# A rebuilt beginning and reordered seams in a four-layer hybrid trunk kernel

## The chip, the cores and the metric

One core of one Trainium2 chip runs the whole step. The metric is device time in microseconds. Before the change the median of three runs is 2044.71 us (2044.56 to 2045.04).

## What is computed

384 tokens of width 1024 (128 context, 256 latent) pass through four layers: pooling mixer, Mamba-2 SSD, Conformer convolution, attention, each followed by a ConvFFN. Each sub-layer is

```python
h = rms_norm(x, g_pre) * (1 + scale) + shift
x = x + gate * rms_norm(mixer(h), g_post)
```

where shift, scale and gate are six vectors of a layer, `silu(cond) @ w_mod + b_mod`, one set for the context tokens and one for the latent ones. The pooling mixer takes, for four groups of 256 columns, the mean over a window of 2, 4, 8 or 16 rows less the row itself, and multiplies each group with a 256 x 256 weight and a scale. Everything is float32.

## The kernel before

Five engines each have their own hand-written list of instructions, tied by semaphores. Tokens stand in three blocks c = 0 (context), 1 and 2 (latent). Matmuls are done in split form: an operand is rounded to fp32r (`w_hi`, `h_hi`) and the rest kept (`w_lo`, `h_lo`), and a product is three matmuls (hi x hi, lo x hi, hi x lo; L1825 to L1827 in `tile`, L1861 to L1863 in `out_part`, L2274 to L2276 in the pooling product). Weights come in chunks of 512 KB into four `raw` slots; ScalarE rounds a chunk (`round_to`, L880), GpSimd (POOL) and VectorE make half of its low part each (`low_to`, L752 and L1267; for conf and qkv weights POOL makes all of it). A chunk number n stands for the first chunk of the next product.

Modulation vectors are made by TensorE from 1 MB pieces, four to a vector (`mod_piece`, L1796), and finished on VectorE (`mod_vector`, `coefficient`). Five vectors are made in the start, three inside ffn_in0 and its transition, three in each later seam (one in the last), where their pieces fill TensorE's time. `FILLS` says how many stand before turn 1 and turn 2.

**Start** (`pool_mix` on TensorE, L1715 to L1757 on VectorE, L1193 to L1217 on ScalarE). `pool_m` holds the window matrices. TensorE multiplies them with ones (`sums`) and then with the normalised rows, one bank for each of eight column groups k, alternating banks 6 and 7. ScalarE scales (L1208), VectorE adds the shift (L1743), ScalarE rounds (L1215), VectorE takes the low part (L1752); `pooled_v` has two buffers. The order of SHIFT0's pieces is behind k = 1, that of GATE0's behind k = 5. The gate coefficients, a 16 x 128 block, are turned to a row by TensorE, copied by ScalarE (`copy_row`), written to HBM (`rows_dram`) and read back into all partitions (`gb`), from ScalarE's queue. Then comes the product and `transition0`.

**Seam t** (t = 0 to 6, the end of sub-layer t; event e = 3t + c). For each block: `first` (square sums of the product, ScalarE), `weigh` (product times gate, L1324; in t = 0 and 4 a scale or bias first, L1319), `residual` (L1333), `second` (square sums of x, L908), `unit` (x normalised, L1340), `turn_unit` (eight transposes on TensorE into pair[3], L1818), `unit_stage` (scale and shift; four groups on ScalarE, L921, four on VectorE, L1352), `unit_high` (L930), `unit_low` (four groups on POOL, L759, four on VectorE, L1360). The lists of all three engines are in `transition` and `transition0`. `in_start` waits for the low parts of all blocks, then tile 0 of the next product starts. SP issues nearly all loads in one queue, in program order, with the waits that free the slots.

## Time and profile before

| | us |
|---|---|
| median of 3 runs | 2044.71 |
| the profiled execution | 2046.58 |
| its span | 2044.8 |
| TensorE busy in it | 1935.7 |
| VectorE, ScalarE, POOL busy | 1191.7, 924.0, 713.5 |

The page cuts the span into 40 slices (51 us each) and gives the busy tenths of each engine:

```profile
PE   6699999999998989999999998899999979899998
PEclk8799999999999989999999999999999989899999
DMA  9764346433330137533374655533365413333342
```

PE is TensorE, PEclk the clock it was granted in tenths of full speed, DMA the busy share of the DMA engines. The first two slices hold the start; the other places below 9 hold the seams and the scan and attention stages. Rows below are of four views: the chain that ended last, the waits, the timeline (start, duration, engine, line, operation, and in brackets the idle time before and what released it) and windows (busy time in chosen stretches, with the clock).

### The profile page before, as it was taken

The page shows a single profiled execution, that of the slowest core. Times are in us where ns is not written, and L with a number is a line of the kernel's source. Part 1 is how long each engine was busy: PE and PEld are TensorE (multiplying, and loading weights), DVE is VectorE, ACT ScalarE, POOL GpSimd, SP SyncE. Part 2 cuts the span into 40 slices and gives each one's busy share as a digit, 9 for nine tenths or more (in the row PEclk, how much of TensorE's full clock was granted, in tenths as well). Part 3 has the DMA queues.
Part 4 walks back from the last instruction along what each step waited for, and adds up shares of the span by engine and source line. Part 5 has one row for each costly group of instructions (what it writes and reads, how often), then busy time and mean ns, then how long its engine had stood idle before and what let it go on. Part 6 is the DMA issues. An engine that isn't in the chain of part 4 may idle for free.

```text
span 2044.8 us, 29870 instructions
## 1 busy us (share of the span) xinstructions
PE 1935.7 (95%) x11679; PEld 1713.0 (84%) x11679; DVE 1191.7 (58%) x1789; ACT 924.0 (45%) x1566; POOL 713.5 (35%) x515
## 2 busy tenths in 40 slices
PE   6699999999998989999999998899999979899998
PEld 3589998799996767999987956899987867799986
DVE  3557761566626675777615844777724684777722
ACT  3444442554546645444424325544424444544422
POOL 0223324333335553333344722333343521333342
PEclk8799999999999989999999999999999989899999
DMA  9764346433330137533374655533365413333342
GB/s 399 319 247 135 124 164 246 169 123 124 97 134 27 48 134 305 187 125 125 116 246 172 207 155 202 211 124 124 113 240 182 174 40 114 112 128 124 124 132 72
DMA packets 80316, 324.29 MB, mean 159 GB/s; under 512 B 9009, under 2 KB 17713, under 8 KB 66609
## 3 DMA queue, kind: packets, MB, share of 16 engines
q1 hardware_dynamic: 78496, 319.42, 44.6%
q10 hardware_dynamic: 1680, 2.96, 0.4%
q8 instruction: 94, 1.54, 0.3%
q14 instruction: 46, 0.37, 0.1%
HBM read 317.24 MB, written 5.10 MB: 158 GB/s over the span
## 4 chain that ended last, share of the span: by engine, by line
PE 81%; DVE 7%; ACT 5%; issue 3%; POOL 2%; DMA 2%; SPq 0%; DVEq 0%; ACTq 0%; POOLq 0%
PE pair L1825 18%; PE pair L1827 17%; PE pair L1826 17%; PE pair L1861 7%; PE pair L1862 7%; PE pair L1863 7%; DVE x L1333 2%; PE pair L1982 2%; PE pair L2076 1%; DMA raw<-in_pool 1%; ACT junk L908 1%; PE pair L1796 1%; DVE wk L1324 1%; PE pair L1987 1%; PE pair L2203 1%
## 5 line engine op out<-in xcount | busy, mean ns | idle before, releaser
L752 POOL TENSOR_TENSOR w_lo<-raw,w_hi 128x512 fp32r<-128x512 f32 (+1 forms) x375 | 587.8, 1569 | 1133.2 <-ACT w_hi L880 1133.1
L1825 PE MATMUL pair<-h_hi,w_hi 128*128 128x386 f32 (+1 forms) x2008 | 687.5, 342 | 13.2 <-POOL h_lo L759 10.5
L1827 PE MATMUL pair<-h_hi,w_lo 128*128 128x386 f32 (+1 forms) x2008 | 682.6, 340 | 0.0
L1826 PE MATMUL pair<-h_lo,w_hi 128*128 128x386 f32 (+1 forms) x2008 | 682.0, 340 | 0.0
L1267 DVE TENSOR_TENSOR w_lo<-raw,w_hi 128x512 fp32r<-128x512 f32 x339 | 411.3, 1216 | 325.5 <-ACT w_hi L880 325.4
L880 ACT ACTIVATE w_hi<-raw 128x1024 fp32r<-128x1024 f32 x375 | 392.9, 1050 | 292.6 <-PE pair L1863 225.6
L1825 PEld LDWEIGHTS pair<-h_hi,w_hi 128*128 128x128 f32 (+1 forms) x2008 | 380.0, 189 | 22.2 <-POOL h_lo L759 16.7
L1826 PEld LDWEIGHTS pair<-h_lo,w_hi 128*128 128x128 f32 (+1 forms) x2008 | 380.5, 189 | 0.9
L1827 PEld LDWEIGHTS pair<-h_hi,w_lo 128*128 128x128 f32 (+1 forms) x2008 | 380.0, 189 | 0.3
L1416 DVE SCALAR_TENSOR_TENSOR acc<-pair,taps,acc 128x385 f32<-128x385 f32 x176 | 108.9, 619 | 207.4 <-ACT acc L984 207.4
L984 ACT ACTIVATE acc<-pair,taps 128x386 f32<-128x386 f32 x176 | 117.3, 666 | 224.7 <-PE pair L1827 224.7
L1862 PE MATMUL pair<-w_hi,g 128*128 128x512 f32 x528 | 208.5, 395 | 0.0
L1863 PE MATMUL pair<-w_lo,g 128*128 128x512 f32 x528 | 208.4, 395 | 0.0
L1861 PE MATMUL pair<-w_hi,g 128*128 128x512 f32 x528 | 208.3, 395 | 0.0
L1861 PEld LDWEIGHTS pair<-w_hi,g 128*128 128x128 f32 x528 | 99.2, 188 | 23.4
L1862 PEld LDWEIGHTS pair<-w_hi,g 128*128 128x128 f32 x528 | 99.2, 188 | 23.3
L1863 PEld LDWEIGHTS pair<-w_lo,g 128*128 128x128 f32 x528 | 99.2, 188 | 23.4
L982 ACT ACTIVATE g<-gate 128x386 fp32r<-128x386 f32 x84 | 44.3, 527 | 163.2 <-DVE gate L1434 163.2
L1423 DVE SCALAR_TENSOR_TENSOR acc<-pair,taps,acc 128x385 f32<-128x385 f32 x176 | 108.5, 617 | 3.2
L1058 ACT ACTIVATE mod_raw<-pair,shift 128x128 f32<-128x128 f32 x192 | 53.7, 378 | 14.3 <-PE pair L1987 14.2
L759 POOL TENSOR_TENSOR h_lo<-stage,h_hi 128x512 fp32r<-128x512 f32 x21 | 32.0, 1522 | 79.5 <-ACT h_hi L930 79.5
L1818 PE MATMUL pair<-ident,wk 128*128 128x128 f32 x168 | 27.0, 313 | 29.9 <-ACT stage L921 12.3
(286 smaller groups left out, 2128.0 us busy)
## 6 DMA issues: line engine op xcount, KB each, us to landing
raw<-in_ffn_in SPq DMA_DIRECT2D x176, 512.0 KB, 3.5
raw<-in_ffn_out SPq DMA_DIRECT2D x88, 512.0 KB, 3.5
mod_raw<-in_w_mod SPq DMA_DIRECT2D x36, 1024.0 KB, 6.8
mod_base<-in_w_mod SPq DMA_DIRECT2D x31, 1024.0 KB, 7.1
mod_more<-in_w_mod SPq DMA_DIRECT2D x18, 1024.0 KB, 20.4
raw<-in_ssd_conv SPq DMA_DIRECT2D x32, 512.0 KB, 3.5
raw<-in_ssd_z SPq DMA_DIRECT2D x16, 512.0 KB, 3.5
raw<-in_ssd_out SPq DMA_DIRECT2D x16, 512.0 KB, 3.8
```

The costliest lines, as they stand in the source:

```text
L752: pool.tensor_tensor(w_lo[:, m % SLOTS, 0:w], raw[:, m % SLOTS, 0:w], w_hi[:, m % SLOTS, 0:w].bitcast(F32), ALU.subtract).then_inc(w_low_p ...
L880: act.activation(w_hi[:, m % SLOTS, 0:w], raw[:, m % SLOTS, 0:w], ACT.Copy).then_inc(w_rounded, 1)
L984: act.activation(acc[:, j % 4, :], tile_bank(j)[:, 0:COLS], ACT.Identity, scale=taps[:, l, j, 1:2], bias=taps[:, l, j, 3:4]).then_inc(acc_ ...
L1267: vec.tensor_tensor(w_lo[:, m % SLOTS, w0:w1], raw[:, m % SLOTS, w0:w1], w_hi[:, m % SLOTS, w0:w1].bitcast(F32), ALU.subtract).then_inc(w_ ...
L1416: vec.scalar_tensor_tensor(out=acc[:, j % 4, 1:COLS], in0=b[:, 0:COLS - 1], scalar=taps[:, l, j, 0:1], in1=acc[:, j % 4, 1:COLS], op0=ALU. ...
L1423: vec.scalar_tensor_tensor(out=acc[:, j % 4, 0:COLS - 1], in0=b[:, 1:COLS], scalar=taps[:, l, j, 2:3], in1=acc[:, j % 4, 0:COLS - 1], op0= ...
L1825: ten.matmul(to, wh, h_hi[:, k, cols], start=k == 0, stop=False, skip_group_check=True)
L1826: ten.matmul(to, wh, h_lo[:, k, cols], start=False, stop=False, skip_group_check=True)
L1827: ins = ten.matmul(to, wl, h_hi[:, k, cols], start=False, stop=k == KD - 1, skip_group_check=True)
L1861: ten.matmul(to, hi[:, k, cols], wh, start=first, stop=False)
L1862: ten.matmul(to, lo[:, k, cols], wh, start=False, stop=False)
L1863: ins = ten.matmul(to, hi[:, k, cols], wl, start=False, stop=last)
```

## The change

Start: `pool_m` keeps only the 136 columns that a block of 128 rows can reach for each latent block (643 columns become 401). Four pooling buffers and four banks (6, 7, 0, 1); rounding and low part of a group come two groups late; ScalarE rounds the pool weights behind four evacuations; SHIFT0's pieces stand behind k = 3, GATE0's behind all groups. The gate row is no longer sent through HBM: TensorE multiplies the gate column, broadcast over 128 columns, with the identity (`spread_gate`), once for each of the two streams, between the thirds of the product, and ScalarE copies the result into `gb`. The product times pool scale of block 2 goes into `h_rows`, dead by then. Turned units of t = 0 go to three different bank pairs. Pieces of vectors 3 and 4 stand around turn 0. SP loads p20 to p23 ahead of the tables.

Seams: POOL makes only the low part of block 0, VectorE all of block 1 and both halves of block 2; block 2 is rounded in halves and tile 0 starts after the first half, its k = 4 waiting for the second; the first chunk's rounding and low part come later in all three lists; `FILLS` changes from (3, 7) to (1, 6).

The core of the diff:

```diff
-POOL_W = LAT0 + 2 * (LAT + 1)
+REACHED = P + max(WINDOWS) // 2
+POOL_W = LAT0 + 2 * REACHED
+POOL_DEPTH = 4
-FILLS = {12: (3, 7), 4: (1, 3)}
+FILLS = {12: (1, 6), 4: (1, 3)}
...
@@ sync @@
             load_to(4)
+            load_ends(0, *range(MOD_PIECES))
             for to, name in ((taps, "taps"), (ssd_taps, "ssd_taps"), (dt_rows, "dt_rows"), (ssd_cols, "ssd_cols")):
...
@@ gpsimd @@
             def transition(t, n):
-                low_to(n + 1)
                 unit_low(t, 0)
-                unit_low(t, 1)
-                low_to(n + 2)
-                unit_low(t, 2)
                 low_to(n + 4)
...
@@ scalar @@
+            def gate_copy(s):
+                act.wait_ge(gate_spread, s + 1)
+                act.activation(gb[:, s, :], pair[3][:, :], ACT.Copy).then_inc(gate_copied, 1)
             def transition0(n):
+                gate_copy(0)
                 first(0, 0)
+                gate_copy(1)
                 first(0, 1)
                 second(0, 0)
                 second(0, 1)
-                round_to(n + 1)
+                first(0, 2)
+                round_to(n + 2)
+                second(0, 2)
                 unit_stage(0, 0)
-                first(0, 2)
                 unit_high(0, 0)
                 unit_stage(0, 1)
-                second(0, 2)
                 unit_high(0, 1)
-                round_to(n + 2)
                 unit_stage(0, 2)
                 unit_high(0, 2)
                 round_to(n + 4)
@@ transition(t, n) @@
                 first(t, 1)
-                round_to(n + 1)
                 unit_stage(t, 0)
                 second(t, 1)
+                unit_high(t, 0)
                 first(t, 2)
-                unit_high(t, 0)
+                unit_stage(t, 1)
                 second(t, 2)
-                unit_stage(t, 1)
                 unit_high(t, 1)
-                round_to(n + 2)
+                round_to(n + 1)
                 unit_stage(t, 2)
...
-            for k in range(KD + 1):
+            for k in range(KD + 2):
                 if k < KD:
                     act.wait_ge(pooled, k + 1)
-                    if k >= 2:
-                        act.wait_ge(pooled_lo, k - 1)
-                    if k == 0:
+                    if k >= POOL_DEPTH:
+                        act.wait_ge(pooled_lo, k - POOL_DEPTH + 1)
+                    if k == POOL_DEPTH:
                         round_to(2)
...
-                if k:
-                    act.wait_ge(pooled_shifted, k)
+                if k >= 2:
+                    act.wait_ge(pooled_shifted, k - 1)
...
@@ vector @@
             def transition0(n):
+                mod_vector(2)
+                coefficient(0, 1)
+                before_weigh(0, 0)
                 weigh(0, 0)
+                before_weigh(0, 1)
+                residual(0, 0)
                 weigh(0, 1)
-                residual(0, 0)
+                residual(0, 1)
+                unit(0, 0)
+                before_weigh(0, 2)
+                unit(0, 1)
                 mod_vector(3)
                 coefficient(0, 2)
+                weigh(0, 2)
+                residual(0, 2)
                 mod_vector(4)
...
+                unit(0, 2)
+                unit_stage(0, 0)
+                unit_stage(0, 1)
+                unit_low(0, 0)
+                unit_low(0, 1)
+                unit_stage(0, 2)
                 low_to(n + 1)
...
                 unit_low(0, 2)
                 low_to(n + 4)
@@ transition(t, n) @@
                 unit(t, 1)
-                low_to(n + 1)
                 weigh(t, 2)
                 residual(t, 2)
+                unit_stage(t, 1)
                 unit_low(t, 0)
-                unit_stage(t, 1)
                 unit(t, 2)
                 unit_low(t, 1)
-                low_to(n + 2)
                 unit_stage(t, 2)
+                low_to(n + 1)
                 unit_low(t, 2)
...
@@ tensor @@
+                def spread_gate(s):
+                    for k in range(KD):
+                        ins = ten.matmul(pair[3][:, k * P:(k + 1) * P], coef[:, 0, 1, s, k:k + 1].broadcast_to([P, P]),
+                                         ident[:, :], start=True, stop=True, skip_group_check=True)
+                    ins.then_inc(gate_spread, 1)
...
-                turn_gate(0)
...
                     if c < 2:
                         ins.then_inc(out_done, 1)
-                ten.wait_ge(pooled_scaled, KD)
-                for p in range(3 * MOD_PIECES, START_VECTORS * MOD_PIECES):
+                        if c == 0:
+                            ten.wait_ge(coef_ready, 2)
+                            ten.wait_ge(pooled_scaled, KD)
+                        else:
+                            ten.wait_ge(gate_copied, 1)
+                        spread_gate(c)
+                for p in range(3 * MOD_PIECES, 4 * MOD_PIECES - 1):
                     mod_piece(p)
-                ten.wait_ge(mod_read, START_VECTORS)
+                ten.wait_ge(gate_copied, 2)
                 turn_unit(0, 0)
+                for p in range(4 * MOD_PIECES - 1, START_VECTORS * MOD_PIECES):
+                    mod_piece(p)
+                ten.wait_ge(pre_ready, 2)
                 turn_unit(0, 1)
+                ten.wait_ge(pre_ready, 3)
                 turn_unit(0, 2)
+                ten.wait_ge(stage_act, 1)
+                ten.wait_ge(stage_dve, 1)
                 fill(0, 0, MOD_PIECES)
```

## Rows read from the trace of the kernel before

**Rows 1.** The page, part 4: share of the chain that ended last, by engine.
```profile
PE 81%; DVE 7%; ACT 5%; issue 3%; POOL 2%; DMA 2%; SPq 0%; DVEq 0%; ACTq 0%; POOLq 0%
```

**Rows 2.** Waits of PE, 0 to 110 us: line, awaited, us in total, times, longest.
```profile
PE pair L1818 <- DVE wk L1340: 10.0, 2, 6.9
...
PE pair L1818 <- DVE stage L1352: 5.3, 1, 5.3
...
PE pair L2274 <- DVE h_lo L1752: 4.1, 1, 4.1
```

**Rows 3.** Waits of PE, 370 to 1800 us.
```profile
PE pair L1818 <- ACT stage L921: 12.3, 5, 4.8
...
PE pair L1825 <- POOL h_lo L759: 10.5, 5, 4.3
...
PE pair L1825 <- DVE w_lo L1267: 2.6, 1, 2.6
```

**Rows 4.** The chain that ended last, up to tile 0: start us, us, what.
```profile
57.14 11.01 DMA gb<-rows_dram
...
69.38 1.23 DVE wk L1319
...
97.84 0.42 PE pair L1825
```

**Rows 5.** Windows: us, busy us by engine, granted clock, DMA share, GB/s.
```profile
85.00:90.00 5.00, 1.94 (x8) 1.57 (x8) 4.93 (x11) 4.13 (x9) 1.20 (x1) 0.50 0.71 295
```

**Rows 6.** Timeline, 24 to 41 us: start us, us, engine, line, [idle before, releaser].
```profile
24.67 0.39 PE L2234 MATMUL pair<-pool_m,ones 128*128 128x129 f32 x2
...
32.20 1.07 PE L1796 MATMUL pair<-mod_more,cond 128*32 128x256 f32 x16 [0.26 <-DMA mod_more<-in_w_mod]
...
38.92 0.74 ACT L1208 ACTIVATE stage<-pair,coef 128x129 f32<-128x129 f32 x2 [0.69 <-DVE h_lo L1752]
...
39.69 0.75 DVE L1743 SCALAR_TENSOR_TENSOR stage<-wk,modc,stage 128x129 f32<-128x129 f32 x2 [0.86 <-ACT stage L1208]
...
40.36 0.55 DVE L1752 TENSOR_TENSOR h_lo<-stage,h_hi 128x386 fp32r<-128x386 f32 x1
...
41.01 0.73 ACT L1208 ACTIVATE stage<-pair,coef 128x129 f32<-128x129 f32 x2 [0.94 <-DVE h_lo L1752]
```

**Rows 7.** Windows of PE alone in the pooling product: us, busy us, clock, DMA share, GB/s.
```profile
53.40:58.00 4.60, 4.60 (x22) 0.50 1.03 429
...
59.00:64.00 5.00, 5.00 (x44) 1.00 1.01 424
```

**Rows 8.** DMA issues at 19.6, 45.6, 46.3, 67.1 us: KB, us to landing.
```profile
mod_more<-in_w_mod SPq DMA_DIRECT2D x1, 1024.0 KB, 24.9
...
mod_raw<-in_w_mod SPq DMA_DIRECT2D x1, 1024.0 KB, 22.5
...
raw<-in_ffn_in SPq DMA_DIRECT2D x1, 512.0 KB, 23.4
...
mod_more<-in_w_mod SPq DMA_DIRECT2D x1, 1024.0 KB, 15.2
```

**Rows 9.** Timeline of the seam t = 1, 384 to 404 us.
```profile
384.06 1.30 POOL L752 TENSOR_TENSOR w_lo<-raw,w_hi 128x512 fp32r<-128x512 f32 x1 [10.74 <-ACT w_hi L880]
...
384.11 2.33 DVE L1333 SCALAR_TENSOR_TENSOR x<-wk,inv,x 128x1024 f32<-128x1024 f32 x1
...
387.89 1.93 PE L1796 MATMUL pair<-mod_raw,cond 128*32 128x256 f32 x32
...
398.99 1.36 DVE L1352 TENSOR_SCALAR stage<-pair,coef,modc 128x128 f32<-128x128 f32 x4
...
401.53 0.69 DVE L1360 TENSOR_TENSOR h_lo<-stage,h_hi 128x512 fp32r<-128x512 f32 x1 [1.19 <-ACT h_hi L930]
...
403.76 0.41 PE L1825 MATMUL pair<-h_hi,w_hi 128*128 128x386 f32 x1 [2.50 <-POOL h_lo L759]
```

**Rows 10.** Windows of PE alone, tile 0 behind the seam t = 2.
```profile
822.80:826.00 3.20, 3.20 (x12) 0.51 0.35 105
```

More of the change, by code:

```diff
@@ L296, in build_trunk @@
         pool_sums = flat_wk[:, 0:len(WINDOWS) * COLS].rearrange("p (g n) -> p g n", g=len(WINDOWS))
-        pooled_v = [flat_stage[:, k * 512:k * 512 + COLS] for k in range(2)]
+        pooled_v = [flat_stage[:, k * 512:k * 512 + COLS] for k in range(POOL_DEPTH)]
         def c_part(v, d, h):
@@ L928, in unit_high @@
                 act.wait_ge(stage_act, e + 1)
-                act.wait_ge(stage_dve, e + 1)
-                act.activation(h_hi[:, :, cols], stage[:, e % 2, :, :], ACT.Copy).then_inc(h_hi_ready, 1)
+                if c < 2:
+                    act.wait_ge(stage_dve, e + 1)
+                    act.activation(h_hi[:, :, cols], stage[:, e % 2, :, :], ACT.Copy).then_inc(h_hi_ready, 1)
+                else:
+                    for half in range(2):
+                        ks = slice(4 * half, 4 * half + 4)
+                        if half:
+                            act.wait_ge(stage_dve, e + 1)
+                        act.activation(h_hi[:, ks, cols], stage[:, e % 2, ks, :], ACT.Copy).then_inc(h_hi_ready, 1)
+            def gate_copy(s):
+                act.wait_ge(gate_spread, s + 1)
+                act.activation(gb[:, s, :], pair[3][:, :], ACT.Copy).then_inc(gate_copied, 1)
             def transition0(n):
+                gate_copy(0)
                 first(0, 0)
+                gate_copy(1)
                 first(0, 1)
@@ L1358, in unit_low @@
                 e, cols = event(t, c), slice(AT[c], AT[c] + P)
-                vec.wait_ge(h_hi_ready, e + 1)
-                vec.tensor_tensor(h_lo[:, 4:, cols], stage[:, e % 2, 4:, :], h_hi[:, 4:, cols].bitcast(F32),
-                                  ALU.subtract).then_inc(h_lo_dve, 1)
+                for half in range(2) if c == 2 else (1,):
+                    ks = slice(0, KD) if c == 1 else slice(4 * half, 4 * half + 4)
+                    vec.wait_ge(h_hi_ready, highs_made(t, c, half))
+                    vec.tensor_tensor(h_lo[:, ks, cols], stage[:, e % 2, ks, :], h_hi[:, ks, cols].bitcast(F32),
+                                      ALU.subtract).then_inc(h_lo_dve, 1)
             def transition0(n):
+                mod_vector(2)
+                coefficient(0, 1)
+                before_weigh(0, 0)
                 weigh(0, 0)
+                before_weigh(0, 1)
+                residual(0, 0)
                 weigh(0, 1)
-                residual(0, 0)
+                residual(0, 1)
+                unit(0, 0)
+                before_weigh(0, 2)
+                unit(0, 1)
                 mod_vector(3)
                 coefficient(0, 2)
+                weigh(0, 2)
+                residual(0, 2)
                 mod_vector(4)
-                residual(0, 1)
-                unit(0, 0)
-                unit(0, 1)
-                low_to(n + 1)
-                weigh(0, 2)
-                unit_stage(0, 0)
-                residual(0, 2)
-                unit_low(0, 0)
-                unit_stage(0, 1)
-                unit(0, 2)
-                unit_low(0, 1)
-                low_to(n + 2)
-                unit_stage(0, 2)
+                unit(0, 2)
[4 more added lines that the diff above has]
+                unit_stage(0, 2)
+                low_to(n + 1)
                 unit_low(0, 2)
@@ L1817, in turn_unit, with tile @@
                 for k in range(KD):
-                    ins = ten.transpose(pair[3][:, k * P:(k + 1) * P], wk[:, e % 2, k * P:(k + 1) * P], ident[:, :])
+                    ins = ten.transpose(turned_pair(t, c)[:, k * P:(k + 1) * P], wk[:, e % 2, k * P:(k + 1) * P], ident[:, :])
                     if k % 4 == 3:
                         ins.then_inc(unit_turned, 1)
-            def tile(to, n, w, cols):
+            def tile(to, n, w, cols, behind=None):
                 for k in range(KD):
+                    if behind is not None and k == 4:
+                        ten.wait_ge(h_lo_dve, lows_on_dve(behind, 2, 1))
                     wh, wl = (v[:, n % SLOTS, k * w:(k + 1) * w] for v in (w_hi, w_lo))
```

201 lines of the change are left out of this document (111 added, 90 removed).

## The prediction

> **What bounds the kernel now.** I read the page first: TensorE carries 81% of the chain that ended last [rows 1]. Inside the stages between the seams it has nothing to wait for, so this change can only win or lose where TensorE stands still or runs slowly. The list of its waits says where. In the first 98 us, before tile 0 of ffn_in0 starts, it waits four times for the work around the pooling mixer and the first transition [rows 2]. Behind that it waits in the six later seams (t = 1 to 6): 12.3 us in five waits before a turn of a unit (L1818), and 10.5 + 2.6 us in six waits before tile 0 of the next product [rows 3]. The chain then tells what ends last at the start: the gate row, written to HBM and read back (the reading alone 11.01 us, to 68.15), so that the first weighing stands until then, and a ping-pong of VectorE and ScalarE up to tile 0 at 97.84 [rows 4]. The DMA engines are full until about 88 us and then idle [rows 5]: they are the second thing to watch.
>
> I number the modulation pieces p0 to p19 (vector i is p4i to p4i+3), p20 to p23 being the first of the next phase.
>
> **The start, step by step.**
>
> Smaller pool_m. Its columns go from 643 to 401, so 1286 KB become 802 KB; the 0.50 MB at about 415 GB/s (295 at a share of 0.71 [rows 5]) bring all later transfers 1.2 us forward. TensorE's matmuls over it get shorter, beside other work: nothing on the path.
>
> Pooling. The last piece of SHIFT0 is used from 32.20 to 33.27 [rows 6] and its vector takes 0.8 more; less 1.2 us, the first shift can run at 32.9. Today the third group is only evacuated at 38.92 [rows 6], because ScalarE rounds two weights first, at the landing of the pool weights, and then each column group k goes evacuation, shift, high part, low part, at 2.1 us a group (38.92 to 41.01, L1208) because there are two buffers [rows 6]. With four buffers and the low part two groups late, the engines overlap. VectorE has 8 x (0.75 + 0.55) + 1.3 for the weights' low part = 11.7 us, ScalarE 8 x (0.74 + 0.52) + 2.1 for two roundings. I followed the order of both: ScalarE is held at h_hi(0) until 33.8, rounds from 35.7 to 37.7, and the rest runs at 1.26 us a group; last low part 46.0, against 53.2 now. Vector 2's pieces on TensorE (p8 to p11) now come behind all groups; p11, issued at 19.6, lands 24.9 later [rows 8], less 1.2 at 43.3, and is used by 44.4: no new wait. Gain so far 7.2 us.
>
> Product and gate. The product's first third ran at a granted clock of 0.50, the 1.2 GHz level: 22 matmuls in 4.6 us, against 44 in 5.0 later [rows 7]. Again 24 at 0.21, 5.1 us, to 51.2. Then spread_gate(0), eight fp32 matmuls of 128 columns. The nearest row is L2234, 129 columns, two records and 0.22 us a matmul [rows 6], so 1.7 us (3.5 at the half clock). Then c = 1 (2.8), spread (1.7), c = 2 (2.8): TensorE is done at 60.5, not 64.1. ScalarE copies the gate from 53.05 (1.05 us), then squares. This replaces the round trip through HBM: the first weighing goes at 55.4 instead of 68.2. What is late next is VectorE's list: before_weigh and weigh 1.23 each [rows 4], and of the same width residual 1.28 with a reciprocal of 0.2, unit 0.95. In the new order that puts unit(0,0) at 63.7 and unit(0,1) at 65.7.
>
> Last column block. SCALE1's vector needs p15 (65.7), weigh(0,2) runs 66.6 to 67.8, residual to 69.2. ScalarE stands in front of second(0,2) with round_to(n+2): the ffn_in0 weights, issued from 46.3, landed near 69.7 and 71 [rows 8]; they are 1.2 us sooner by pool_m and 2.5 us by the row of 1 MB that is no longer written to gb, so 66 and 67.3, rounded by 68.7. So second(0,2) runs 69.25 to 70.7, unit(0,2) is ready at 71.7. SHIFT1 needs p19, issued at 45.6 and landed at 68.1 now [rows 8], 64.5 after: its vector is made at 70.0, not last. VectorE then does unit_stage(0,0) to 73.0, stage(0,1), the low parts and stage(0,2), a stage 1.36, a low part of four groups 0.69 [rows 9], ending 79.2, the moved low part of chunk n to 79.9, the first half of unit_low(0,2) at 80.5. Tile 0 at 80.6 against 97.84: 17.2 us.
>
> DMA order. p20 to p23 are now queued ahead of the tables; p21 still waits on SP until p12 is used, and behind SP stand tables and weights n+2 and n+3. p23, issued at 67.1, landed at 82.3 [rows 8]; without 2.0 MB ahead of it (pool_m, gb, tables) it lands near 77 and TensorE has used it at 78. Cover is 2.5 us; later than that, tile 0 starts one for one later. The weights for tile 2 land near 80, needed at 89.
>
> Clock. TensorE is now paced by DMA from 72.8 to 78 and idle to 80.6. Where TensorE was mostly idle the granted clock was 0.50 [rows 5], and the product behind it had its first third at that level [rows 7], which cost it 24 x 0.09 = 2.2 us. Today tile 0 follows on pieces that run without a gap. I charge it what the product paid, a little up: 2.5. Start: 17.2 - 2.5 = 14.7 us. Bounds: 17.2 with a warm clock; 9 if the p19/p23 landings or ScalarE's order cost 3 to 5 us more.
>
> **The seams t = 1 to 6.** The change takes the low part of c = 1 from POOL wholly to VectorE (+0.65 us there), halves the last high and low part so tile 0 starts after the first half, takes the rounding of chunk n from before unit_stage(t,0) to behind unit_high(t,1), and gives turn 1 one fill piece in place of three. I take t = 1 as the pattern [rows 9]. VectorE's residual took 2.33 us beside POOL's w_lo [rows 9] and 1.28 alone: 1.05 us back. unit_stage(0) runs at 385.3, not 386.4; unit(2) is ready at 394.65, not 395.5. Then: unit_low(1) with 8 groups to 395.9, unit_stage(2) to 397.2, low part of chunk n to 397.9, half a low part to 398.55. VectorE and ScalarE would let tile 0 go at 398.6 against 403.76. But TensorE has its own work from the product's end at 387.89: 15.87 us passed to tile 0, of which 2.94 were waits, so 12.9 us of pieces and turns. With 0.3 for the one short gap left before turn 2 it is ready at 401.1. So the bound changes from POOL's h_lo to TensorE itself, and such a seam gives its waits less 0.3, not the 5 us of the chain: t = 1 2.6; and, with the waits of [rows 3] split by seam, t = 3 (3.0 us of waits) 2.7; t = 5 (3.1) 2.8; t = 2 (3.5) 3.2. At t = 2 the granted clock was 0.51 in the first 3.2 us of tile 0, behind the wait [rows 10]; half of that, 1.7 with the edges, goes too if the wait goes: 4.9.
>
> t = 4 is longer because a bias is added first: unit(2) comes at 1283.6 instead of 1285.8, turn 2 still waits 2.4 us and turn 1 1.5, then six pieces: tile 0 at 1290.1, not 1294.1; less 0.5 for clock: 3.5. t = 6 has only four pieces (phase 7 is one vector), so the chain itself counts: 5.1 us; the clock of its tile 0 I leave as it is. Sum of seams 2.6 + 4.9 + 2.7 + 3.5 + 2.8 + 5.1 = 21.6 us. Bounds: 14 (clock unchanged, another 0.7 us gap a seam) to 25.
>
> What is moved, and its cover. POOL's w_lo of n and n+1 come later (396.8 and 400.6 in the t = 1 pattern); tile 0 is at 401.1, tile 1 4.3 us on. For conf_in and qk POOL makes the whole 1024 columns, 2.4 us a chunk, still under 4.3 us a tile. Pieces 9 to 11 of a seam are loaded into slots that pieces 0 to 2 free; piece 2 is used at 391.7, 1.1 us later than now, lands some 7 us behind and is needed at 400.2: 1.3 us of cover. Row indices, semaphores and psum banks cost nothing.
>
> The Trainium skill, SBUF — State Buffer (Who interferes with whom), says that a VectorE instruction with two SBUF inputs and a GpSimd one exclude each other for a whole instruction. The residual beside w_lo (2.33 against 1.28) agrees. That rule also speaks against the change: unit_low(t,1) on VectorE and w_lo of chunk n on POOL now meet at 395.5. By it VectorE loses up to 1.3 us there; in five seams TensorE's own 12.9 us hide that, in t = 6 they don't, and the sum would be 1.3 us smaller.
>
> **The sum.** 14.7 + 21.6 = 36.3 us. The profiled execution took 2046.58 with a span of 2044.8; the median of the runs is 2044.71. Against the span 2008.5, and I take the same for the median.
>
> **Rivals.**
> A. The start stays tied to DMA: p19 or p23 lands 4 to 6 us later than I count, or ScalarE's roundings hold second(0,2) for longer. For: DMA share is 1.0 throughout, and SP's queue stands behind matmuls [rows 5, 8]. Against: 2 MB less ahead. Start 9, seams 21.6: 2014.
> B. The seams give almost nothing, because the turns wait again: new order on ScalarE puts unit_high(0) before first(2) (1.05 us) and second(2) behind unit_stage(1). If that comes back as wait at turn 2, only start and 5 us remain: 2025. Against: unit(2) has 0.3 us to lose and TensorE 2.5 us of slack at the end.
> C. Clock. The seams' and the start's tile 0 run warm, with all chain gains: 17.2 + 25: 2002. Against: the clock of 0.50 from 80 us on [rows 5], with the same idle stretches ahead. The Trainium skill, TensorE: Matmul & The Clock Gate (What's actually happening), has the clock halved after idling; the trace agrees.
> D. Slower: VectorE becomes the bound in the seams. It gets 0.65 us of low part, and each meeting with POOL costs 1.05 to 1.3. It decides once a seam's chain, 398.6 by my count, ends later than 403.76, and to eat the start too it must be 2.5 us beyond that in all six: 7.6 us more VectorE time a seam, six meetings with POOL where I see one. It would give 2050.
> E. Nothing happens, gains and losses cancel: 2044.7.
>
> **Chances.** Forecast (2004 to 2013) 0.60; A 0.17; B 0.10; C 0.08; D 0.03; E 0.02. The range takes in A, C and the near part of B: 1999 to 2023. A measurement of this kernel can tell 0.2% (4 us) from none: faster 0.95, same 0.02, slower 0.03.
>
> **What would show it.** Right: no gb transfer at the start; first weigh (now L1324) near 55; tile 0 of ffn_in0 near 80 with 0.32 us between matmuls first; in seams 1, 2, 3, 5 no wait before tile 0 and a TensorE-bound seam of some 13.2 us; in t = 6 a start 5 us nearer to the product's end. Wrong: TensorE waiting for DMA on a piece just before tile 0, a wait of over 1 us before turn 2, or VectorE rows of 2 us in the seams.

## The result and the profile after

| | median | runs | profiled span | granted clock |
|---|---|---|---|---|
| before | 2044.88 | 2044.56 to 2046.06 | 2044.8 | 0.976 |
| after | 2007.79 | 2007.7 to 2008.61 | 2006.0 | 0.985 |
| forecast | 2008.5 | range 1999 to 2023 | | |

All in us. The ratio is 0.9818 with a 95% interval of 0.9801 to 0.9836: 37.1 us less by the medians and 38.8 by the spans, where 36.3 had been forecast. (The median of before in this table is over four runs: the three named at the beginning and one more.)

TensorE's share of the chain that ended last is up from 81% [rows 1] to 87%. Page of the changed kernel, part 4:

```profile
PE 87%; DVE 5%; ACT 2%; issue 2%; DMA 2%; POOL 1%; SPq 0%; DVEq 0%; POOLq 0%; ACTq 0%
```

TensorE's waits in the changed kernel, the answers to [rows 2] (0 to 110 us) and to [rows 3] (350 to 1800 us); columns: line, awaited, us in total, times, longest:

```profile
PE pair L1870 <- DVE wk L1388: 2.0, 2, 1.7
PE pair L1879 <- DVE h_lo L1409: 1.8, 1, 1.8
```

```profile
PE pair L1870 <- DVE wk L1388: 8.7, 8, 2.8
...
PE pair L1879 <- DVE h_lo L1409: 0.9, 1, 0.9
```

Lines have moved: the turn of a unit is now L1870 (L1818 before), the first matmul of a product L1879 (L1825), a modulation piece L1848 (L1796). In the seams TensorE had 25.4 us of waits in eleven places [rows 3], and 2.1 more in three for VectorE's wk, not shown there. They have become 9.6 in nine, and the wait for POOL's h_lo ahead of tile 0 is gone: the only one left there is 0.9 us, for VectorE, in the seam t = 6.

The span splits at the first matmul of each phase's tile 0 (each row from one profile). This ledger sets the forecast's terms beside what came:

| stretch, ending with tile 0 of | before | after | gained | forecast |
|---|---|---|---|---|
| start to ffn_in0 | 97.84 | 79.76 | 18.1 | 17.2 |
| ssd_conv (t = 1) | 305.92 | 305.13 | 0.8 | 2.6 - 2.5 |
| ffn_in1 (t = 2) | 418.79 | 415.75 | 3.0 | 3.2 |
| conf_in (t = 3) | 298.17 | 294.10 | 4.1 | 2.7 + 1.7 |
| ffn_in2 (t = 4) | 173.38 | 170.58 | 2.8 | 3.5 |
| qk (t = 5) | 296.44 | 293.82 | 2.6 | 2.8 |
| ffn_in3 (t = 6) | 165.17 | 160.29 | 4.9 | 5.1 |
| the end | 289.09 | 286.57 | 2.5 | 0 |

The seams themselves can be cut out more narrowly, from TensorE's first modulation piece behind the product to tile 0. For t = 1 to 6 that was 15.9, 16.4, 15.9, 20.8, 16.0 and 15.8 us, and is 13.6, 13.5, 13.6, 18.1, 13.4 and 11.4: 17.4 us less in all. What the stretches behind the start gain beyond that, 3.3 us, is put down to the clock and to the scatter of a profile.

The start of the changed kernel, the last part of the chain of work up to tile 0 (start us, us, what); the columns of [rows 4]:

```profile
45.75 0.55 PE pair L2326
50.36 1.78 PE pair L2292 x16
54.96 1.80 PE pair L2292 x16
...
78.46 0.60 DVE w_lo L1300
79.06 0.61 DVE h_lo L1409
79.76 0.54 PE pair L1879
```

The 11 us of reading gb back [rows 4] are no longer there; two spreads of 1.8 us by TensorE (L2292) stand in their place, and VectorE's last list ends last.

### The profile page after: what moved, and what is told of

It reads as the page before. It is cut to its first block, busy times and chain, and to the rows that moved or that the text cites. A ratio compares the mean times of both kernels' runs of the same rounds, so it can differ in the third digit from the quotient of the medians.

```text
span 2006.0 us, 29908 instructions
## 1 busy us (share of the span) xinstructions
PE 1927.0 (96%) x11710; PEld 1705.9 (85%) x11710; DVE 1183.8 (59%) x1796; ACT 927.1 (46%) x1574; POOL 692.1 (35%) x501
## 4 chain that ended last, share of the span: by engine, by line
PE 87%; DVE 5%; ACT 2%; issue 2%; DMA 2%; POOL 1%; SPq 0%; DVEq 0%; POOLq 0%; ACTq 0%
PE pair L1879 18%; PE pair L1881 18%; PE pair L1880 18%; PE pair L1911 8%; PE pair L1912 8%; PE pair L1913 8%; PE pair L1848 2%; PE pair L2032 2%; PE pair L2126 1%; DMA mod_base<-in_w_mod 1%; DMA pool_m<-in_pool_m 1%; PE pair L2253 1%; PE pair L2037 1%; PE pair L1870 1%; PE pair L2046 1%
## 5 line engine op out<-in xcount | busy, mean ns | idle before, releaser
L1879 PE MATMUL pair<-h_hi,w_hi 128*128 128x386 f32 (+1 forms) x2008 | 686.6, 342 | 2.7 <-DVE h_lo L1409 2.7
L1300 DVE TENSOR_TENSOR w_lo<-raw,w_hi 128x512 fp32r<-128x512 f32 x339 | 405.8, 1200 | 325.3 <-ACT w_hi L908 325.2
L1879 PEld LDWEIGHTS pair<-h_hi,w_hi 128*128 128x128 f32 (+1 forms) x2008 | 378.9, 189 | 11.5 <-issue 10.1
L1037 ACT ACTIVATE xbc<-pair,ssd_taps 128x386 f32<-128x386 f32 x32 | 21.6, 674 | 72.7 <-PE pair L1881 72.7
L1486 DVE TENSOR_TENSOR gate<-sil,acc 128x386 f32<-128x386 f32 x88 | 53.8, 611 | 0.0
```

The lines of the kernel that those rows point to most:

```text
L1300: vec.tensor_tensor(w_lo[:, m % SLOTS, w0:w1], raw[:, m % SLOTS, w0:w1], w_hi[:, m % SLOTS, w0:w1].bitcast(F32), ALU.subtract).then_inc(w_ ...
L1879: ten.matmul(to, wh, h_hi[:, k, cols], start=k == 0, stop=False, skip_group_check=True)
```

## The experiments

All are edits of the changed kernel. "By segment" means the stretches of the ledger, each from one profile. Kernels that share a start had tile 0 of ffn_in0 anywhere from 79.5 to 81.1 us, so that a single start is good to about 1 us.

### Start or seams

The start as changed, and for t of 1 and up the old order on all three lists and the old shares (VectorE's list, changed back in the same way, is not shown):

```
+ if t == 0: unit_low(t, 0)
+ else: low_to(n + 1); unit_low(t, 0); unit_low(t, 1); low_to(n + 2); unit_low(t, 2)      (GpSimd)
+ round_to(n + 1)                                              (ScalarE, before the seam's first unit)
- FILLS = {12: (1, 6), 4: (1, 3)}
+ FILLS = {12: (3, 7), 4: (1, 3)}
```

> The new beginning with the old seams t = 1 to 6 (lists of all engines, POOL's share, whole last block, FILLS (3, 7)). My theory: the two halves of the change add up, the start being worth 38.8 us minus the 22.4 us that the traces give to the seams: 2044.8 - 16.4 = 2028.4 us, with the old waits of TensorE before turn 2 and tile 0 back (some 27 us in all with turn 0 and 1). Rival (the seams give little, and the start all): 2010 to 2015. Rival (a slower rounding of tile 0's weights shifts loads, so that the parts don't add): off the sum by over 3 us.

Measured: 2026.96 (ratio 0.9916, interval 0.990 to 0.993; span 2027.4). So the start is worth 17.9 us and the seams 19.2 by medians, 17.4 and 21.4 by spans; forecast 14.7 and 21.6. (The profiled execution was the slowest of the four, 2.2 us above their median.) Most of the old waits are back, 22.7 of the 25.4 us:

```profile
PE pair L1879 <- ACT stage L955: 12.3, 5, 4.8
PE pair L1888 <- POOL h_lo L791: 10.4, 5, 3.8
```

(TensorE's waits of this kernel, 350 to 1800 us; compare [rows 3].)

### The start: four buffers, narrow pool_m, gate row

```
- POOL_DEPTH = 4
+ POOL_DEPTH = 2                          (and the low part one group late, not two)
```

> The changed kernel with two pooling buffers and two banks, rounding and low part one group late as before; all else of the new beginning stays. My theory: a group takes 2.1 us again instead of 1.1 to 1.3, from the third or fourth on, so the product starts 5 to 6 us later (near 51 instead of 45.75) and, since VectorE and ScalarE end last from there to tile 0, nearly all of it reaches tile 0 (84 to 86 instead of 79.76): 2012 to 2014 us. Rival (the DMA landings p19 and p23 end last, so the buffers were worth little): within 2 us of the changed kernel.

Measured: tile 0 at 84.26, 4.5 us later; median 2009.82. The whole is only 2.0 us slower, since the stretch to ffn_in1 came out 2.2 us shorter by TensorE's clock (below).

```
- REACHED = P + max(WINDOWS) // 2
+ REACHED = LAT + 1
- POOL_LAT = [(LAT0, LAT0), (LAT0 + REACHED, COLS - REACHED)]
+ POOL_LAT = [(LAT0, LAT0), (LAT0 + REACHED, LAT0)]
```

> The changed kernel with pool_m at 643 columns again. 0.5 MB more are loaded ahead of most of the start. My theory: all landings come 1.2 us later; the first shifts and the product wait for p7 and start about 1 us later, tile 0 about 1 us: 2009 us. Rival (cover on the DMA side is thin, p23 lands behind the low parts): over 2 us. Rival (no effect, a chain that doesn't touch the loads): below 0.3.

Measured: tile 0 at 82.92, 3.2 us later; median 2010.20. The rival's "over 2" came, but not by the late landing that it named. TensorE's timeline between 20 and 36 us, the wide kernel first and then the changed one (start us, us, engine, line, operation):

```profile
20.97 0.80 PE L2283 MATMUL pair<-pool_m,ones 128*128 128x129 f32 x2 [5.27 <-DMA pool_m<-in_pool_m]
...
28.57 1.03 PE L2286 MATMUL pair<-pool_m,h_rows 128*128 128x257 f32 x4
...
31.72 3.66 PE L1848 MATMUL pair<-mod_more,cond 128*32 128x256 f32 x64
```

```profile
19.88 0.80 PE L2283 MATMUL pair<-pool_m,ones 128*128 128x129 f32 x2 [4.42 <-DMA pool_m<-in_pool_m]
...
26.25 0.63 PE L2286 MATMUL pair<-pool_m,h_rows 128*128 128x136 f32 x4
...
28.19 3.83 PE L1848 MATMUL pair<-mod_more,cond 128*32 128x256 f32 x64
```

pool_m lands 1.1 us later, and the four pieces of SHIFT0 start 3.5 us later, without any wait for a DMA: the other 2.4 us are matmuls. With the wide matrix a group's second part takes 1.03 us, not 0.63, and four groups stand ahead of those pieces, with the window sums.

The gate row written to HBM and read back, in the new order of everything else (TensorE turns the block ahead of the product in place of spread_gate; not shown):

```
- act.activation(gb[:, s, :], pair[3][:, :], ACT.Copy).then_inc(gate_copied, 1)
+ act.dma_start(rows_dram[7:8, :]..., grow[:, 0, :]).then_inc(gate_stored, 16)
+ act.wait_ge(gate_stored, 16)
+ act.dma_start(gb[...], rows_dram[7:8, :].broadcast_to([P, 2 * D])).then_inc(gate_back, 16)
```

> The changed kernel with the gate row sent through HBM again: TensorE turns the 16 x 128 block ahead of the product, ScalarE copies, writes, waits and reads back, no spread_gate. My theory: the row is back at about 63.5 us (write 5.4, read 11), weigh(0,0) goes then instead of at 54.37, and 7 to 9 us reach tile 0: 2014 to 2017 us. Rival (the start is paced by the DMA landings of pieces and weights, the gate row was hidden by them): 2.5 us, the time of its 1 MB.

Measured: tile 0 at 88.94, 9.2 us later; median 2016.64. Its chain of work shows where (start us, us, what):

```profile
47.73 4.58 DMA rows_dram<-grow
52.34 10.32 DMA gb<-rows_dram
```

The row is back at 62.7 us, where the changed kernel weighs at 54.4. These two parts and pool_m, undone alone, cost 4.5 + 3.2 + 9.2 = 16.9 us at tile 0, against 17.4 us for the whole start by the spans. Parts undone one at a time need not add up, so that little seems left for the rest of the start, but that was not tested.

Thirteen matmuls with no use for their result, before tile 0 of ffn_in0:

```
+ def keep_busy(to, count):
+     for _ in range(count):
+         ten.matmul(to[:, 256:384], ident[:, :], ident[:, :], start=True, stop=True, ...)
- fill(0, 0, MOD_PIECES)
+ fill(0, 0, MOD_PIECES - 1); keep_busy(bank(6), 6); fill(0, MOD_PIECES - 1, MOD_PIECES); keep_busy(bank(6), 7)
```

> The changed kernel with 13 matmuls more (128 columns, results used by nobody) in the two gaps of TensorE before tile 0 at the start: 6 ahead of p23, 7 behind it. My theory: the granted clock, 0.5 for 3.4 us from 79.4 on, stays at 1.0, and tile 0 is 1.7 us shorter at the same start: 2006.1 us. Rival (the clock fell for what TensorE did earlier, or the added matmuls delay p23 or tile 0): same or slower than the changed kernel.

Measured: 2006.88, tile 0 at 80.34. Windows of the first 3 us of tile 0, the changed kernel and then this one (us, PE busy, granted clock, DMA share, GB/s):

```profile
79.80:82.80 3.00, 3.00 (x10) 0.52 1.03 436
```

```profile
80.40:83.40 3.00, 3.00 (x19) 1.00 1.03 426
```

Ten matmuls against nineteen in the same 3 us, at 1.2 and at 2.4 GHz. The next stretch fell from 305.13 to 303.42, so the low clock had cost 1.7 us. That the idle matmuls prevented it is not shown. Two kernels below, with an unchanged start and none of these matmuls (the early rounding and the old shares), also had tile 0 at the full clock behind a wait of 1.4 us (1.8 in the changed kernel). A window of 3 us just behind its start, of the early rounding (it reads 1.00 for the old shares too):

```profile
79.80:82.80 3.00, 3.00 (x19) 1.00 1.01 426
```

Their next stretch was short too, 303.95 and 303.51 us. In these two and in the kernel with the idle matmuls the clock had been low from about 71 to 75 us instead, ahead of the first idle matmul (76.2 us). So of eight kernels with an unchanged start six had tile 0 at the low clock and two did not; both kernels with idle matmuls had it at the full one.

### The seams: order, shares, fills, load

```
- FILLS = {12: (1, 6), 4: (1, 3)}
+ FILLS = {12: (3, 7), 4: (1, 3)}
```

> The changed kernel with FILLS back at (3, 7): three pieces before turn 1 and seven before turn 2. My theory: in t = 1, 2, 3 and 5 TensorE's own work of 12.9 us ends last whatever its order, so nothing is lost there; at t = 4 one of the waits (1.27 and 2.25 us) takes a piece and some 1 us is gained. 2006 to 2008 us. Rival (the new number of pieces is what removed the waits): turn 1 and turn 2 come later, VectorE and ScalarE end last again, 1 to 2.5 us a seam: 2013 to 2018.

Measured: 2006.87. The seams t = 1, 3, 5 each came out 0.3 to 0.6 us shorter, and the stretch to ffn_in1 by 2.8, by the clock. The end was 1.8 longer, by the clock again. The new boundaries of the fills gain nothing: from first piece to tile 0 the five seams t = 1 to 5 take 69.1 us with the old ones, 72.1 with the new.

The rounding of chunk n's first weights back to before the seam's first unit, and GpSimd's low part of it first:

```
+ low_to(n + 1)              (GpSimd, t >= 1, ahead of unit_low(t, 0))
+ round_to(n + 1)            (ScalarE, ahead of the seam's first unit)
```

> The changed kernel with ScalarE's rounding of chunk n back behind first(t,1), and POOL's low part of it ahead of unit_low(t,0). All else as changed. My theory: residual(t,1) again runs beside POOL's low part and takes 2.3 us instead of 1.28; unit_stage(0) and unit(1) come 1 us later; TensorE's work hides most of it in t = 1, 2, 3, 5 and t = 4 and 6 lose up to 1 us each: 2008 to 2010. Rival (the place of the rounding is what the seams gained by): 2.5 us a seam, 2020.

Measured: 2013.97 (2012.0 to 2015.02), 6.2 us slower by the medians; TensorE's waits for VectorE before a turn went from 8.7 to 14.0 us. Both the theory (2008 to 2010) and the rival (2020) missed it. By segment: -1.2 at t = 1 (by the clock of tile 0 before it), +1.4 at t = 3, +1.7 at t = 5, +0.6 at t = 6 and +2.1 in the end, by the clock of its tile 0: 4.3 in this profile, which is the fastest of four runs. From first piece to tile 0 the six seams are 4.6 us longer. The reason stands in the timeline of the seam t = 3 of this kernel, and under it the same residual in the changed kernel:

```profile
1075.76 2.40 POOL L784 TENSOR_TENSOR w_lo<-raw,w_hi 128x1024 fp32r<-128x1024 f32 x1 [10.74 <-ACT w_hi L910]
1075.82 3.43 DVE L1382 SCALAR_TENSOR_TENSOR x<-wk,inv,x 128x1024 f32<-128x1024 f32 x1
```

```profile
1077.34 1.28 DVE L1379 SCALAR_TENSOR_TENSOR x<-wk,inv,x 128x1024 f32<-128x1024 f32 x1
```

The residual takes 1.28 us alone and 3.43 where GpSimd's w_lo began 0.06 us ahead of it and ran for 2.40: it stands nearly until GpSimd is done.

GpSimd's old share of the low halves in the new order (the first four groups of unit 1 and all of unit 2's, so that the two halves of the last unit go too):

```
+ if t: unit_low(t, 1); low_to(n + 1); unit_low(t, 2)                          (GpSimd)
- for half in range(2) if c == 2 else (1,):
+ for half in range(2) if c == 2 and t == 0 else (1,):                         (VectorE)
```

> The changed kernel, but in every seam from block 1 on GpSimd takes back the share of the low halves that it had before the change (the first four groups of each unit and all of the last block), still in the new order of the seam; the start is as changed. Theory (what the new order gained is the order of the pieces on TensorE, and VectorE's load is hidden): the same time within 1 us in the seams of blocks 1, 2, 3 and 5, about 2 us more in block 6, so about 2010. Rival (the share that VectorE took over is itself the gain, since the residual is no longer waiting behind GpSimd): about 2 us more in each of six seams, 2018 to 2020.

Measured: 2011.18 (2008.49 to 2014.78), where the changed kernel, built again and run beside it, gave 2008.36 (2007.6 to 2011.49): the two overlap. By segment, against that one: nothing at t = 1 to 3 that isn't the clock's (-1.5, -2.1, 0), +1.5 at t = 4, +0.4 at t = 5, +2.0 at t = 6 and +1.6 in the end by its clock. The 1.5 lie ahead of the seam t = 4: from its first piece to tile 0 it takes 18.2 and 18.0 us, while between 1195 and 1215 us the clock was 0.74 here and 0.83 there. At t = 6 TensorE's wait before tile 0 is 2.52 us in place of 0.93 (timeline of this kernel):

```profile
1719.85 0.44 PE L1883 MATMUL pair<-h_hi,w_hi 128*128 128x386 f32 x1 [2.52 <-POOL h_lo L791]
```

The residual kept its mean of 1285 ns over the seams, so the share did not lengthen it as the rival said. So the shares and the halving decide in the short seam t = 6, with some 1.5 us from first piece to tile 0, and are worth 0.4 us at most elsewhere.

Two reductions of 1024 columns put into VectorE's list in every seam, that nobody waits for:

```
+ for i in range(2):
+     vec.tensor_reduce(ballast[:, 2 * t + i:2 * t + i + 1], x[:, 0, :], AX.X, ALU.max)
```

> The changed kernel with two reductions over 1024 columns (about 1.1 us each) added on VectorE in each seam t = 1 to 6, between unit(t,2) and unit_low(t,1). Their result is read by nobody. My theory: t = 1, 2, 3, 5 end with TensorE's pieces and have some 2.4 us of slack on VectorE, so they hide it, t = 4 nearly; only t = 6, which has four pieces, pays 2.2: about 2010 us, with tile 0 of t = 6 2.2 us later behind turn 2 and the others within 0.3. Rival (VectorE bounds all seams): 6 x 2.2 = 13 us, 2021.

Measured: 2012.17 (2008.66 to 2013.39), over the 2010 of the theory and far from the rival's 2021. 2.3 us more on VectorE lengthened t = 1 to 5 by 0.7 at most and t = 6 by 1.2; the end grew by another 1.5, by the clock of its tile 0 (window of PE alone, 0.67 in the first 5.2 us), and 1.3 came before tile 0 of ffn_in0, within the scatter of starts. So VectorE has about 2 us of slack in five of six seams, 1.6 at t = 1.

### What the gaps of t = 4 were worth, and all together

```
- fills = FILLS[len(end_pieces(t))]
+ fills = (2, 9) if t == 4 else FILLS[len(end_pieces(t))]
```

> The changed kernel with more filler matmuls of the mixer's own work placed between the turns of the seam of block 4 alone: boundaries after 2 and 9 pieces in place of 1 and 3. Theory: the three gaps of that seam in the changed kernel (1.15, 1.27 and 2.25 us on TensorE) come from turns that wait for VectorE with too little behind them; they close, and the segment that ends with block 4's tile 0 falls by about 3.5 us from 170.6, all else equal: about 2004.5. Rival: the gaps only move to where the pieces were taken from, same time within 1 us.

Measured: 2002.83 (2002.19 to 2005.13), 5.5 us below the changed kernel beside it. Not all of it is this edit's: the stretch of t = 4 fell from 170.20 to 166.23, 4.0 us, and the one to ffn_in1, which the edit leaves alone, from 416.61 to 413.52 by the clock. (The expectation names the old boundaries wrongly: this seam has twelve pieces, and its boundaries were 1 and 6.) TensorE's timeline of that seam, the changed kernel first:

```profile
1249.56 1.09 PE L1870 MATMUL pair<-ident,wk 128*128 128x128 f32 x8 [1.27 <-DVE wk L1388]
1250.58 1.07 PE L1848 MATMUL pair<-mod_raw,cond 128*32 128x256 f32 x16
1251.47 3.64 PE L1848 MATMUL pair<-mod_base,cond 128*32 128x256 f32 x64
1257.36 1.88 PE L1870 MATMUL pair<-ident,wk 128*128 128x128 f32 x8 [2.25 <-DVE wk L1388]
```

```profile
1247.86 1.09 PE L1870 MATMUL pair<-ident,wk 128*128 128x128 f32 x8 [0.40 <-DVE wk L1388]
1248.88 6.25 PE L1848 MATMUL pair<-mod_base,cond 128*32 128x256 f32 x112
1255.67 1.09 PE L1870 MATMUL pair<-ident,wk 128*128 128x128 f32 x8 [0.54 <-DVE wk L1388]
```

A seam with a bias ahead of its weighing has a longer chain on VectorE between two turns; seven pieces fit in there, where five had been put. The turn itself also ran at the low clock (1.88 us) behind the 2.25 us gap and at the full one (1.09) behind 0.54.

> The changed kernel with three additions: 13 idle matmuls (their result is not used) that keep TensorE busy while it waits for tile 0 of block 0; the boundaries 2 and 9 in the seam of block 4 and the older boundaries 3 and 7 in the others; and ten such idle matmuls before the last turn in the seam of block 6. Theory: minus 1.7 us in the first segment after tile 0 (the clock stays at 0.98), minus 3.5 in block 4, minus 0.5 in block 6, and plus or minus 0.6 a seam for the boundaries: 2001 to 2003. Rival (the clock falls elsewhere in the SSD scan or the last block when the phase shifts): 2005 to 2007.

Its edit is that of e7 and e8 together, FILLS (3, 7) elsewhere, and ten idle matmuls before the last turn of t = 6. Measured: 2000.45 (1999.25 to 2002.0), ratio to before 0.979 (0.9775 to 0.9804): 7.9 us below the changed kernel beside it, its range wholly below, and 0.6 below what was expected. By segment, against that one: -1.9 (t = 1), -1.4, -0.2, -4.0 (t = 4), -0.8, -0.3, 0. The ten idle matmuls of t = 6 thus gave no more than the scatter (0.3 us). This is the best kernel of the study.

> The changed kernel, unchanged, for the spread of a program that is built again: 2007.8 within 0.6 us, tile 0 of block 0 at 79.5 to 81, and the half-clock stretches near 601 and 704 us either both there, as in the first profile, or both absent, which would put the segment that holds them 2 to 3 us lower and the whole at about 2005. If they are the same as before, their place is set by the program; if not, by the run.

Measured: 2008.36 (2007.6 to 2011.49), before beside it 2043.29 (2041.05 to 2046.43). No segment of its profile is over 0.9 us from that of the first, and both half-clock stretches are there again. As only one execution of each build was profiled, that does not yet say that the program sets their place (last section).

## Why the prediction held, step by step

**The sum.** 36.3 us forecast, 37.1 by the medians, 38.8 by the spans. The terms of the ledger say how much of that closeness is luck. Short by 0.9 at the start, by 0.8 for the clock of the first tile 0 and by 2.5 for the end; over by 0.1 to 0.7 in each seam, 1.7 together. The mechanisms stood, the errors partly cancelled. (The arithmetic of rival D doesn't hold: 2.5 us in each of six seams would eat the start and give 2045, not 2050. It changed nothing in the forecast.)

**The start as a whole.** Forecast tile 0 at 80.6, measured 79.76. Along the way: first shift 32.9 and 32.78; product 46.0 and 45.75; first weighing 55.4 and 54.37; unit(0,2) at 71.7 and 70.82 (the turn that waits for it); last modulation piece from DMA 77 and 76.93; the weights for tile 2 near 80 and 79.5. Each stood on a list of one engine counted from durations of before, and each came within 1.1 us. The start's gain at tile 0, 18.1 us, was under-forecast by 0.9. Spreading the gate took 1.78 and 1.80 us for 1.7. The undoing of the gate row alone gave 9.2 us, that of the four buffers 4.5: both mechanisms are shown.

**Smaller pool_m: this step was wrong.** It said 1.2 us by DMA, and of the shorter matmuls "beside other work: nothing on the path". The DMA part is right (1.1 us). But the change also puts four groups, not two, ahead of SHIFT0's pieces on TensorE, and so the shorter matmuls count, 2.4 us: 3.2 in all at tile 0. The forecast of the first shift did not suffer, because it was taken from the old place of the last piece of SHIFT0 [rows 6], where only two groups had stood ahead: the narrow matmuls pay for the two that were moved in front. Two omissions cancelled there. Of a step that is moved, what it now stands ahead of has to be counted too.

**Clock of the first tile 0.** Forecast a low clock and 2.5 us; the clock was 0.52 and cost 1.7. The product had paid 24 matmuls of 0.09 us; here the low clock lasted from 79.9 to 83.3, ten matmuls of 386 columns at 0.32 us in place of 0.18. That tile 0 would run at the low clock was right for this kernel, and the size of the term was off. That it must, behind this idle stretch, is not shown: two kernels with the same start didn't. The product's own first third was forecast at the low clock for its whole 4.6 to 5.1 us; window of PE alone in the changed kernel, beside [rows 7]:

```profile
45.75:50.36 4.61, 4.61 (x26) 0.63 1.00 412
```

**The seams t = 1, 3, 5.** "The bound changes from POOL's h_lo to TensorE itself" was the core of it and is right. Forecast some 13.2 us from the end of the product to tile 0 without a wait before it; at t = 1 it was 371.34 to 384.89, 13.55. From first piece to tile 0 these three seams gained 2.3, 2.3 and 2.6 us, for 2.6, 2.7 and 2.8 forecast: the 0.3 allowed for a gap was a little short. Rows of the seam t = 1 of the changed kernel, for [rows 9]:

```profile
367.56 1.28 DVE L1379 SCALAR_TENSOR_TENSOR x<-wk,inv,x 128x1024 f32<-128x1024 f32 x1
...
371.34 1.07 PE L1848 MATMUL pair<-mod_raw,cond 128*32 128x256 f32 x16
...
377.96 1.22 DVE L1409 TENSOR_TENSOR h_lo<-stage,h_hi 128x1024 fp32r<-128x1024 f32 x1
378.10 1.09 PE L1870 MATMUL pair<-ident,wk 128*128 128x128 f32 x8 [0.21 <-DVE wk L1388]
...
378.79 1.53 POOL L784 TENSOR_TENSOR w_lo<-raw,w_hi 128x512 fp32r<-128x512 f32 x1 [6.21 <-ACT w_hi L908]
...
383.89 1.07 PE L1848 MATMUL pair<-mod_base,cond 128*32 128x256 f32 x16 [0.24 <-DMA mod_base<-in_w_mod]
384.89 0.44 PE L1879 MATMUL pair<-h_hi,w_hi 128*128 128x386 f32 x1
```

The residual is at its 1.28 us, the wait before the last turn is 0.21 (forecast 0.3), and tile 0 follows without one. One bound was drawn too well: the last piece was given 1.3 us of cover by a landing "some 7 us behind". It is issued at 375.36 and used at 383.89, 8.5 us later, with a wait of 0.24 (0.3 to 1.0 in other seams and kernels). The cover was gone. Rival D, VectorE as the bound, is refuted with room: 2.3 us more on it cost 0.7 at t = 1 and 0.2 at most in the other four.

**t = 2 and 3.** The seam t = 2 was forecast to gain 3.2 and gained 3.0, from first piece to tile 0 (16.4 to 13.5 us) as well as by the stretch; the second agreement alone would prove little, since the clock in the scan moves that stretch by 2 to 3 us (last section). The stretch of t = 3 was forecast at 2.7 + 1.7 for the clock of tile 0, and gained 4.1. The 3.2 us behind the seam t = 2 ran at 0.51 [rows 10] and now at 1.00 (window of PE alone):

```profile
800.70:803.90 3.20, 3.20 (x20) 1.00 0.66 179
```

Twelve matmuls then, twenty now: the low clock went with the wait, as said. In all twelve kernels with the new seams this tile 0 ran at 1.00, in the two with the old ones at 0.55 and 0.64 over its first 3 us.

**t = 4.** 3.5 forecast, 2.8 measured. The waits left were named and right (2.4 and 1.5 us forecast, 2.25 and 1.27 measured); a third of 1.15 before turn 0, which was there before the change too (1.16), hadn't been named. What the forecast did not see is that they could be filled: 4 us more.

**t = 6.** 5.1 forecast, 4.9 measured. The seam itself gained 4.4 (15.8 to 11.4). VectorE's chain counts there more than in any other seam, which the extra load and the old shares both show (+1.2 and +2.0).

**The end: the step that was left out.** "The clock of its tile 0 I leave as it is" was worth 2.5 us, the largest miss of the sum. Windows of the first 5.2 us of tile 0 of ffn_in3, before and after:

```profile
1755.80:1761.00 5.20, 5.20 (x17) 0.50 0.42 143
```

```profile
1719.50:1724.70 5.20, 5.20 (x30) 1.00 0.57 202
```

The reasoning of t = 2 could have been applied, since the wait before this tile 0 fell from 4.3 to 0.9 us. But it is no sure gain: the end cost 288.1 to 288.7 us again with the extra load, the old rounding and the old shares, and also with the old fills and the gate by HBM (288.4 each), which leave the load of that seam as it is. Two builds of the changed kernel and five variants stayed at 286.5 to 286.6. The gaps alone don't say which it will be. TensorE's last turn and tile 0 of the seam t = 6, in the changed kernel and then in the one with the old fills:

```profile
1714.79 1.93 PE L1870 MATMUL pair<-ident,wk 128*128 128x128 f32 x8 [2.80 <-DVE wk L1388]
1719.43 0.42 PE L1879 MATMUL pair<-h_hi,w_hi 128*128 128x386 f32 x1 [0.93 <-DVE h_lo L1409]
```

```profile
1711.81 1.09 PE L1870 MATMUL pair<-ident,wk 128*128 128x128 f32 x8 [2.80 <-DVE wk L1388]
1715.61 0.66 PE L1879 MATMUL pair<-h_hi,w_hi 128*128 128x386 f32 x1 [0.85 <-DVE h_lo L1409]
```

Behind the same gap of 2.80 us the low clock fell on the turn in the first (1.93 for 1.09) and left tile 0 alone; in the second it spared the turn and fell on tile 0 (0.66 for 0.42). What decides between them is open.

**Which part of the new order gains.** Of the 17.4 us that the six seams gained from first piece to tile 0, the place of the rounding accounts for 4.6 (undone alone), the shares and the halving for 2.5, the fills for none. By medians it is 6 and 3 of 19.2. The other 10 or so were not taken apart further; that they come from the rest of the order (high, stage and low parts of the units ahead of the weights' low parts on GpSimd and VectorE) is argued, not shown.

**The lock of the shared port.** The Trainium skill, SBUF — State Buffer (Who interferes with whom), was weighed with a loss of 1.3 us for VectorE at t = 6, where unit_low(t,1) meets GpSimd's w_lo. They met, and VectorE lost nothing. At t = 1 its low part of 1024 columns took 1.22 us (rows above) though GpSimd's w_lo began in its midst; it was GpSimd's that took 1.53, where beside the one-input reductions of the extra load it took 1.28. At t = 6 the two took 1.22 and 1.51. The group of the residual over all seams says what the lock had cost (the mean in ns is the number behind the busy time):

```profile
L1333 DVE SCALAR_TENSOR_TENSOR x<-wk,inv,x 128x1024 f32<-128x1024 f32 x18 | 34.4, 1913 | 0.9 <-DVE inv L1307 0.3
```

```profile
L1379 DVE SCALAR_TENSOR_TENSOR x<-wk,inv,x 128x1024 f32<-128x1024 f32 x18 | 23.1, 1284 | 0.6
```

Before, then after, 350 to 1800 us: 0.63 us off each of 18 on average. Undoing the place of the rounding alone brought the mean back to 1694, undoing the shares alone left it at 1285. The same section of the Trainium skill says that whoever issues first keeps the port for the whole instruction. The trace agrees: GpSimd 0.06 us ahead made 3.43 of 1.28, VectorE 0.8 us ahead stayed at its own time. The prediction used only that the two exclude each other, and priced the loss without asking who is first.

## What to carry to other kernels

Where an engine's low-priority work (ScalarE's rounding of the next weights) wakes another engine (GpSimd), it decides which instruction of a third (VectorE) has to wait: place it so that the critical engine's two-input instruction begins first. A gap of TensorE costs more than its length if the clock behind it falls; filling it with the kernel's own pieces gave 4 us at t = 4. When an added instruction seems to have kept the clock, look whether kernels without it kept it too. When a step is moved ahead of others, count what it now delays, not only what it waits for; and when the bound has moved to TensorE, look at each remaining gap for work that is only placed a turn too late.

## What the runs showed of the hardware that was not expected

TensorE stands for about 2.6 us at the start of the SSD scan in every kernel, waiting for GpSimd. Whether the clock falls behind that gap differs. Windows of PE alone just after it, of the changed kernel, of the same kernel built again, and of the one with the old fills:

```profile
601.00:605.00 4.00, 3.42 (x10) 0.64 0.10 35
```

```profile
601.00:605.00 4.00, 3.45 (x9) 0.63 0.08 28
```

```profile
601.50:605.50 4.00, 3.47 (x16) 1.00 0.19 66
```

The gap ended at 601.32 us in the first and at 601.57 in the third, with the same length (2.59 and 2.60). The same holds near 704 us. Where both ran at the full clock (old fills, two buffers, gate by HBM, fills at t = 4, old shares) the stretch to ffn_in1 took 412.9 to 414.5 us; where both ran low (six kernels with these seams) 415.7 to 416.6. So the clock in the scan alone moves a kernel's time by 2 to 3 us, 0.1%, and an experiment whose effect is that small must be read by segment.

What decides it is open. It is not simply where the gap stands. The clock behind it was low in kernels whose gap ended at 599.8, 600.2, 601.3, 601.3, 603.3, 604.2 and 605.45 us, and full where it ended at 599.2, 599.5, 601.6, 602.0, 605.50 and 611.7. Nor is it shown to belong to the program, with one profile of each build; the four runs of one build spread by up to 3 us (2002.19 to 2005.13 with the fills at t = 4). The Trainium skill, TensorE: Matmul & The Clock Gate (What's actually happening), says that the gate judges activity by a clock of its own that doesn't start with the kernel. A low clock that falls on one kernel and spares the next behind the same gap agrees with it. By that the two builds of the changed kernel met the low clock at the same places by chance, which no run here tests.
